# One expert layer's token rows: from selection products to a DRAM buffer and transposes

## The reference, cut to what matters

```python
def moe_swiglu(h, router, wg, wu, wd):
    logits = (h @ router).astype(jnp.float32)
    top_vals, top_idx = lax.top_k(logits, TOP_K)          # TOP_K = 2
    gates = jax.nn.softmax(top_vals, axis=-1)
    gate_e = jnp.sum(jax.nn.one_hot(top_idx, N_EXPERTS) * gates[..., None], axis=-2)
    out = jnp.zeros_like(h)
    for e in range(N_EXPERTS):                            # 8 experts, D_FF = 3584
        out = out + gate_e[..., e:e + 1] * swiglu(h, wg[e], wu[e], wd[e])
    return out
```

## Time and profile before

| | us |
|---|---|
| median of 3 runs | 2628.06 (2624.84 to 2633.0) |
| span of the profiled execution | 2626.9 |
| PE busy | 2533.8 |
| DVE busy | 1814.5 |
| ACT busy | 1450.9 |
| mean DMA rate over the span | 240 GB/s |

### The profile page before, as it was taken

The page is one execution under the profiler, slowest core; times in us unless marked ns, Lnnn a source line. Parts: engine busy times, 40 slices in busy tenths (PEclk is TensorE's granted clock), DMA queues, the critical chain, the costliest instruction groups (busy, mean ns, idle before and its releaser), DMA issues.

```text
span 2626.9 us, 33515 instructions
## 1 busy us (share of the span) xinstructions
PE 2533.8 (96%) x11951; PEld 2014.9 (77%) x11951; DVE 1814.5 (69%) x1779; ACT 1450.9 (55%) x1613; POOL 51.7 (2%) x40
## 2 busy tenths in 40 slices
PE   7999999889999999999999999999999999998998
PEld 6678887667888888888888787888884688777787
DVE  6565446648898989888888985645444575777544
ACT  4553434647777777676767775445433343466443
POOL 0000000000000000000000000600000000000000
PEclk9999999989999999999999999999999999999999
DMA  6865543759999999999999996655534344435661
GB/s 218 310 222 187 189 162 107 262 185 385 348 361 344 360 347 358 340 365 335 372 335 369 325 344 208 226 189 186 188 132 137 95 131 133 133 106 170 200 192 64
DMA packets 327742, 631.65 MB, mean 240 GB/s; under 512 B 14088, under 2 KB 112936, under 8 KB 327464
## 3 DMA queue, kind: packets, MB, share of 16 engines
q1 hardware_dynamic: 326792, 627.35, 68.7%
q0 software_dynamic: 864, 3.15, 0.3%
HBM read 629.40 MB, written 1.05 MB: 240 GB/s over the span
## 4 chain that ended last, share of the span: by engine, by line
PE 87%; DVE 6%; ACT 4%; issue 2%; DMA 1%; SPq 0%; DVEq 0%; ACTq 0%
PE ps L904 21%; PE ps L830 19%; PE ps L934 11%; PE ps L859 9%; PE ps L1304 6%; PE ps L764 5%; PE ps L1331 2%; PE ps L1236 2%; DVE As L2302 1%; PE ps L959 1%; PE ps L1039 1%; PE ps L919 1%; PE ps L843 1%; PE ps L1295 1%; ACT As L1696 1%
## 5 line engine op out<-in xcount | busy, mean ns | idle before, releaser
L2302 DVE TENSOR_TENSOR As<-ringA,As 128x2048 fp32r<-128x2048 f32 x318 | 732.9, 2305 | 224.8 <-ACT As L1613 131.9
L904 PE MATMUL ps<-As,xgs 128*128 128x512 f32 x2688 | 660.7, 396 | 5.7 <-DVE As L2302 3.0
L904 PEld LDWEIGHTS ps<-As,xgs 128*128 128x128 f32 x2688 | 495.0, 188 | 112.0 <-issue 5.8
L1696 ACT ACTIVATE As<-ringA 128x2048 fp32r<-128x2048 f32 x224 | 428.8, 1914 | 28.3 <-PE ps L904 28.1
L830 PE MATMUL ps<-As,xs 128*128 128x512 f32 x1456 | 377.8, 398 | 3.9 <-DVE hh L2339 3.9
L934 PE MATMUL ps<-Bs,hds 128*128 128x512 f32 x1332 | 322.9, 391 | 4.7 <-DVE hds L2365 1.9
L830 PEld LDWEIGHTS ps<-As,xs 128*128 128x128 f32 x1456 | 273.2, 190 | 63.6 <-DVE hh L2339 4.8
L934 PEld LDWEIGHTS ps<-Bs,hds 128*128 128x128 f32 x1332 | 248.2, 188 | 63.0 <-issue 9.7
L2384 DVE TENSOR_TENSOR Bs<-ringB,Bs 128x2048 fp32r<-128x2048 f32 x111 | 254.0, 2289 | 7.3 <-ACT Bs L1726 4.9
L859 PE MATMUL ps<-Bs,hds 128*128 128x512 f32 x1056 | 247.9, 390 | 0.0
L1726 ACT ACTIVATE Bs<-ringB 128x2048 fp32r<-128x2048 f32 x111 | 213.1, 1920 | 62.1 <-PE ps L934 62.1
(11 more groups left out here) (390 smaller groups left out, 3276.9 us busy)
## 6 DMA issues: line engine op xcount, KB each, us to landing
ringA<-in_moe_w_gate SPq DMA_DIRECT2D x112, 1024.0 KB, 5.1
ringA<-in_moe_w_up SPq DMA_DIRECT2D x112, 1024.0 KB, 5.2
ringB<-in_moe_w_down SPq DMA_DIRECT2D x112, 1024.0 KB, 5.4
ringA<-in_w_ff_in SPq DMA_DIRECT2D x132, 512.0 KB, 4.7
ringA<-in_w_in SPq DMA_DIRECT2D x56, 1024.0 KB, 5.3
ringA<-in_w_ada SPq DMA_DIRECT2D x36, 1024.0 KB, 6.2
ringB<-in_w_ff_out SPq DMA_DIRECT2D x33, 1024.0 KB, 5.0
ringA<-in_dense_w_gate SPq DMA_DIRECT2D x28, 512.0 KB, 3.7
```

The source lines that it names most:

```text
L904: m = mm(ps[:, bank, :], lhs(l, tt, k), As[:, h, r, k % 4, :], start=k == 0 and n == 0, stop=k == KC - 1 and n == 2)
L1696: A(As[:, h, 0, :, :], ringA[:, (p["a"] + u) % 2, 4 * h:4 * h + 4, :], ACT.Copy).then_inc(A_high, 1)
L2302: V.tensor_tensor(As[:, h, 1, :, :], ringA[:, (p["a"] + u) % 2, 4 * h:4 * h + 4, :], f32(As[:, h, 0, :, :]), ALU.subtract).then_inc(A_spli ...
```

## The change

The chosen rows of experts 1 to 7 are no longer computed. A DRAM buffer `taken` holds (8 + 1) * 128 rows of 1024. POOL fills it with zeros by nine DMAs, behind the first layer's attention (`o_done` at 4). In expert 0's block 3, DVE works out in `places` for each token and each of its two choices the row `e * 128 + slot`, and POOL then writes the token rows there by four indirect DMAs (2 choices, 2 tiles). SP waits for these (`put`) once, in expert 0. In experts 0 to 6, behind the loads of pair i = 3, SP loads the next expert's 128 rows into `xrow`, which is `xn[:, 0, :]`. At the gather's old place PE turns these rows with 8 transposes. Expert 0's own rows are still made by the products. `one_hot` for `sel` is done for expert 0 alone.

```diff
         most = sb("most", [P, 1], I32)
+        place = sb("place", [P, 2 * TILES], U32)
+        taken = nc.dram_tensor("taken", ((NE + 1) * P, D), F32, kind="Internal").ap()
         AR_N = 18688
...
         chosen = ar(2816, TILES, NE)
+        xrow = xn[:, 0, :]
+        blank = ar(18192, 256)
         sgW, hhW = (hT[:, k:k + 4, :].rearrange("p k n -> p (k n)").rearrange("p (t n) -> p t n", t=TILES) for k in (0, 4))
...
         slot_mm, most_ready, col_ready, sel_ready, selg_ready = (sem(n) for n in ("slot_mm", "most_ready", "col_ready", "sel_ready", "selg_ready"))
+        cleared, placed, put, rows_back = (sem(n) for n in ("cleared", "placed", "put", "rows_back"))
         gathered, xg_ready, selg_tp, selgT_ready, mixed_back, added = (sem(n) for n in ("gathered", "xg_ready", "selg_tp", "selgT_ready", "mixed_back", "added"))
...
                     for h in range(2):
-                        if isinstance(e, int) and isinstance(i, int) and i == 0:
+                        if isinstance(e, int) and e == 0 and isinstance(i, int) and i == 0:
                             half_free(a0, h)
...
-                def rest(e):
-                    with sp.Fori(1, nb // 2) as i:
+                def pairs_of(e, first, last):
+                    with sp.Fori(first, last) as i:
                         for u in range(2):
...
+                def rows_of_next(e):
+
+                    sp.wait_ge(tile_done, e * (2 * nb) + (p["td"] + 2))
+                    sp.dma_start(xrow, taken[bass.ds(e * P + P, P), :]).then_inc(rows_back, 16)
+
+                def rest(e):
+                    pairs_of(e, 1, 4)
+                    if isinstance(e, int) and e == 0:
+                        sp.wait_ge(put, 16 * 2 * TILES)
+                    rows_of_next(e)
+                    pairs_of(e, 4, nb // 2)
+
+                def start(e):
+                    for u in range(2):
+                        A(e, 0, u)
+                        B(e - 1, nb // 2 - 1, u)
+
...
                 rest(0)
-                with sp.Fori(1, NE) as e:
-                    for u in range(2):
-                        A(e, 0, u)
-                        B(e - 1, nb // 2 - 1, u)
+                with sp.Fori(1, NE - 1) as e:
+                    start(e)
                     rest(e)
+                start(NE - 1)
+                pairs_of(NE - 1, 1, nb // 2)
                 B(NE - 1, nb // 2 - 1, 0)
...
-            def gather(e):
-
-                pe.wait_ge(sel_ready, e + 1)
-                if not isinstance(e, int) or e >= 2:
-                    pe.wait_ge(added, 2 * e - 2)
+            def gather_first():
+
+                pe.wait_ge(sel_ready, 1)
                 for half in range(2):
...
                             last = mm(ps[:, 6 + half, k * P:(k + 1) * P], xn[:, tt, o:o + P], sel[:, tt, :], start=tt == 0, stop=tt == TILES - 1)
+                    last.then_inc(gathered, 1)
+
+            def turn_taken(e):
+
+                pe.wait_ge(rows_back, 16 * e)
+                if not isinstance(e, int) or e >= 2:
+                    pe.wait_ge(added, 2 * e - 2)
+                for half in range(2):
+                    for k in range(4):
+                        o = (4 * half + k) * P
+                        last = tr(ps[:, 6 + half, k * P:(k + 1) * P], xrow[:, o:o + P], ident)
                     last.then_inc(gathered, 1)
...
                         if not final:
-                            gather(e + 1)
+                            turn_taken(e + 1)
...
             with pe.If(pe.value_load(most[0:1, 0:1], min_val=0, max_val=SEQ) < CAP + 1):
-                gather(0)
+                gather_first()
                 expert(0)
...
+            ch.done(G.memset(blank, 0.0))
+            pool.wait_ge(o_done, 4)
+            for g in range(NE + 1):
+                pool.dma_start(taken[g * P:(g + 1) * P, :].rearrange("p (a b) -> p a b", a=4), blank.unsqueeze(1).broadcast_to([P, 4, 256])).then_inc(cleared, 16)
             pool.wait_ge(vt_copied, 1)
...
+            pool.wait_ge(cleared, 16 * (NE + 1))
+            pool.wait_ge(pn_xn, PN["ffn1"]["xn"] + 2)
+            pool.wait_ge(placed, 4)
+            for j in range(2 * TILES):
+                pool.indirect_dma_start(out=taken[:, :], out_offset=bass.IndirectOffsetOnAxis(ap=place[:, j:j + 1], axis=0), in_=xn[:, j % 2, :], in_offset=None).then_inc(put, 16)
             pool.wait_ge(spread_copied, units_before(NADA))
...
                 all_tokens(NE - 1)
+                act.wait_ge(rows_back, 16 * (NE - 1))
                 for h in range(2):
...
+            def places():
+
+                at, hit, to = small[:, 400:416].rearrange("p (t e) -> p t e", t=TILES), small[:, 416:448].rearrange("p (j e) -> p j e", j=2 * TILES), small[:, 448:452]
+                for tt in range(TILES):
+                    last = V.scalar_tensor_tensor(at[:, tt, :], k1("iota")[:, 0:NE], float(P), slots[:, :, tt], ALU.mult, ALU.add)
+                last.then_inc(placed, 1)
+                dve.wait_ge(placed, 1)
+                for j in range(2 * TILES):
+                    last = V.scalar_tensor_tensor(hit[:, j, :], k1("iota")[:, 0:NE], ixf[:, j % 2, j // 2:j // 2 + 1], at[:, j % 2, :], ALU.is_equal, ALU.mult)
+                last.then_inc(placed, 1)
+                dve.wait_ge(placed, 2)
+                V.tensor_reduce(to, hit, X, ALU.add).then_inc(placed, 1)
+                dve.wait_ge(placed, 3)
+                V.tensor_copy(place[:, :], to).then_inc(placed, 1)
+
...
                         add(e - 1, 0)
+                    if n == 3 and first:
+                        places()
                     if n == 4:
...
                             dve.wait_ge(selg_tp, e)
-                        one_hot(e, 2 * e + 2, True)
-                    if n == 5 and not final:
-                        dve.wait_ge(gathered, 2 * e + 2)
-                        one_hot(e + 1, 2 * e + 3, False)
+                        one_hot(e, e + 2, True)
                     if n == NB1 - 2 and not final:
...
             with dve.Else():
+                places()
+
```

## The result

| | before | after |
|---|---|---|
| median of 6 runs each, us | 2631.78 (2624.84 to 2635.82) | 2612.11 (2607.39 to 2618.61) |
| span of the profiled execution | 2626.9 | 2606.0 |
| PE busy | 2533.8 | 2511.2 |
| DVE busy | 1814.5 | 1811.8 |
| POOL busy | 51.7 | 67.0 |

The ratio is 0.9936 with a 95% interval of 0.9920 to 0.9952: 16.8 us less, between 12.6 and 21. The prediction said 13.3 us less.

The account below looks back on a forecast made before the run. PE was taken as the bound, busy 96% of the span, with DVE and the DMA engines close. 17.3 - 2.5 - 0.5 - 1.0 = 13.3 us less turned the median of 2628.06 into 2614.8 us, range 2608 to 2625.

Parts of the forecast that it names:

- seven boundaries: At the gathers of experts 1 to 7, transposes replacing products save 2.47 us each, 17.3 us in all.
- row loads: Each expert's 0.52 MB load delays SP's later weight loads 1.36 us, hidden by the ring's lead: 0, uncovered 9.5 us.
- clearing: Nine zeroing DMAs behind the first attention partly meet the first dense loads: 2.5 us lost, bounds 0 and 3.6.
- `places`: Eight short DVE instructions behind expert 0's block 3: 0.5 us lost, bounds 0 and 1.6.
- `put`: SP's wait in expert 0 for the indirect writes holds up the weight loads queued behind it: 1.0 us lost.
- DVE's two idle spells: At each gather, DVE's idle 1.16 us (hidden tile) and 1.31 us (weight part) go when PE is earlier.
- the DMA stream is the real bound: Rival: loads over the experts set the pace, leaving a gain of 3.8 us, 2624.3 us; chance 0.09.
- 3.5 MB in the free time: Of the clearing's 4.7 MB, the part that moves in free DMA time from 128 to 145 us.
- `put` somewhat late: Rival: POOL's four indirect issues in expert 0 wait behind DVE, `put` 9.2 us later, 2624.0 us; chance 0.11.
- the lead of 7.4: Time in us from a weight load's landing to its need, by which loads can be late without costing PE.
- the slower rival: Slow indirect DMA issues in expert 0 hold SP at `put`; at 15 us each the kernel takes 2648; chance 0.07.
- DVE keeps its place: Rival: at the gathers DVE's idle for ACT stays, leaving 4.1 us gained, 2624.0 us; chance 0.05.
- The change doesn't do what it says: Rival: the kernel takes the branch for all tokens, so the edited gather isn't the one run; no own chance given.

Follow-up runs that it names:

- run 9: Changed kernel, clearing moved behind the dense stage with seven DMAs, and expert 0's wait for `put` and row load two pairs later: 2610.4 us, ratio 0.9931.
- runs 2 to 6: Changed kernel with, in order: selection products kept, 2633.0 us; later clearing, 2607.51; two transposes, 2613.78; `dispatch` on ACT, 2619.61; these last two together, 2612.67.
- run 1: Kernel before, with transposes of the first 128 rows replacing experts 1 to 7's products and none of the new DMAs: 2607.04 us, ratio 0.9930.
- run 8: Changed kernel with three, in another kernel seven, further 0.52 MB DMAs behind each row load: 2617.24 us with three, 2656.55 us with seven.
- run 7: Changed kernel, with POOL waiting for seven more blocks of the expert layer before its indirect DMAs: 2628.3 us.

## Why the prediction was right, step by step

| step | predicted, us | measured, us |
|---|---|---|
| seven boundaries | -17.3 (2.47 each) | -19.0 (2.72 each) |
| row loads | 0 | 0 (125.15 to 125.19 with, 125.13 to 125.23 without) |
| clearing | +2.5 | +2.7 (2.1 to 3.3 at expert 0's first product) |
| `places` | +0.5 | at most +0.55 (expert 0 of run 9 less before) |
| `put` | +1.0 | +1.1 (after less run 9, expert 0; 0.3 to 1.5 with the others) |
| sum | -13.3 | -14.6 |

`places` and `put` each rest on one execution of run 9. Six kernels run the same expert 0 (after, runs 2 to 6), and it takes 109.19 to 110.42 us in them, so the two terms together are 0.8 to 2.1 us, where 1.5 was predicted.

**The boundary.** The mechanism held: PE's product time leaves, DVE's two idle spells close, and the release by `xgs` moves by 15.60 - 12.96 = 2.64 us. The size was a little low on both sides. Eight transposes followed by a product hold PE for 0.79 us, not 0.88 (two with their tail) or 1.04 (the last one's end counted), so PE gives 2.70. On DVE, two spells of 1.16 and 1.31 make 2.47, but when nothing is idle between two instructions they also overlap by some 0.08 us each (697.08 + 0.41 = 697.49, yet the next starts at 697.41), which makes 2.64. An idle spell in the trace is a little shorter than what closing it returns. The period gives 2.72 us; where the last 0.08 lie wasn't found. That the missing `one_hot` is worth nothing wasn't tested by itself: it went together with the products in every run.

**The loads.** That the row loads cost nothing is shown by runs 1, 2 and 8. The rival "the DMA stream is the real bound" falls, though the share now reads 1.00: a share of 1.00 at 366 GB/s still left room for four times the row load, and the stream became the bound at 378 GB/s (run 8).

The Trainium skill (DMA: Bandwidth & Descriptors, "Issuing engines are not separate DMA queues") has all issuers on the same 16 engines. The trace agrees: POOL's clearing made a load of SP's 2.7 us later. The landings tell it too; while the indirect writes ran, from 619 to 632 us, these are issues and the time from issue to landing:

```profile
ringA<-in_moe_w_up SPq DMA_DIRECT2D x2, 1024.0 KB, 10.7
ringB<-in_moe_w_down SPq DMA_DIRECT2D x1, 1024.0 KB, 11.5
```

Before it was 5.3 us.

**The clearing.** 3.5 MB in the free time were predicted. The queues from 128 to 145 us (packets, MB, share) show POOL's:

```profile
q0 software_dynamic: 972, 3.58, 53.0%
```

The other 1.1 MB met the first dense load.

**`put`.** The term came out right, by two errors that cancel. I had priced the issue of an indirect DMA by a plain one, 0.77 us, so 3.1 us for four. They took 9.0 us (619.64 to 628.64). The rival "`put` somewhat late" had named just this, with 9.2 us on top; 5.9 came. But the delay of the stream was overstated. I had it 9.4 us late from 628.25 on, although in my own working POOL was through with its issues at 620.8; that left 7.4 us in which the data could move, and the late issues fell into them. By 628.6, the end of the last issue, 0.62 of the 2.1 MB had moved. In run 9, where SP isn't held at this place, the load in question goes out 628.11 - 578.70 = 49.4 us behind expert 0's first product, before the change 628.25 - 579.45 = 48.8, and after it 637.99 - 580.78 = 57.2 us: 7.8 to 8.4 us late, little more than the lead of 7.4. So the size of this term is luck: 5.9 us of late issue cost next to nothing of their own, and run 7 shows that the next ones would have. The price of the slower rival at 15 us an issue, 2648, doesn't follow from its own steps either: `put` at 677.7 is 42 us behind 635.7, 14.3 of them are gained elsewhere, and 2628.06 + 27.7 = 2655.8.

**DVE keeps its place** fell with the two idle spells. **The change doesn't do what it says** fell with the rows of 8 transposes.

**What stays open.** The measured parts sum to -14.6 us and the ratio gives -16.8 us; the 2.2 us between them are inside the interval. Whether they come from the clock's lower level, whose stretches lie elsewhere in every run, wasn't tried. What such a stretch costs can be estimated: from the first dense load to expert 0's first product, run 1 has 428.43 us with 17.1 at the lower level, run 9 433.50 with 30.7, and neither has the clearing ahead, so it is 0.37 us for each. By that the 6.9 us behind the experts make 2.6 of the profiled pair's 4.9; the rest is open too.

## What to carry to other kernels

Read a step's price on every engine that has to pass the same point. Here DVE's own run and the way through PE and ACT stood within 0.07 us of each other once the gather was short, and a further cut on PE or on DVE alone bought nothing. A busy DMA stream is not yet a bound: the lead of the ring, read as the time from landing to need, says how large a burst is free, as long as the stream as a whole has room; and a share of 1.00 doesn't say whether it has. And where an effect of 3 us is looked for in a kernel whose runs spread by 10, compare the parts in the trace, not the medians.

## What the runs showed of the hardware

**An indirect DMA's issue waits for DVE's splits.** DVE's timeline beside POOL's four issues above:

```profile
618.99 2.28 DVE L2343 TENSOR_TENSOR As<-ringA,As 128x2048 fp32r<-128x2048 f32 x1
621.46 2.29 DVE L2343 TENSOR_TENSOR As<-ringA,As 128x2048 fp32r<-128x2048 f32 x1 [0.19 <-ACT As L1736]
624.26 2.29 DVE L2425 TENSOR_TENSOR Bs<-ringB,Bs 128x2048 fp32r<-128x2048 f32 x1 [0.51 <-ACT Bs L1766]
...
627.76 2.29 DVE L2343 TENSOR_TENSOR As<-ringA,As 128x2048 fp32r<-128x2048 f32 x1
```

These splits end at 621.27, 623.75 and 626.55; the issues end at 622.24, 624.60 and 627.38, so 0.97, 0.85 and 0.83 us behind. The fourth issue begins at 627.69, just ahead of the next split, and takes 0.95 us. In run 7 the issues fall elsewhere, and the fourth begins inside a split that ends at 648.56:

```profile
638.66 2.33 POOL L1541 DMA_INDIRECT taken<-xn,place  x1 [102.36 <-DVE As L2344]
641.29 2.93 POOL L1541 DMA_INDIRECT taken<-xn,place  x1 [0.30 <-issue]
644.53 2.66 POOL L1541 DMA_INDIRECT taken<-xn,place  x1 [0.30 <-issue]
647.49 1.90 POOL L1541 DMA_INDIRECT taken<-xn,place  x1 [0.30 <-issue]
```

It takes 1.90 us there, until 649.39, again 0.83 us behind the split's end; the other three end 0.96, 0.85 and 0.83 us behind theirs. So an issue is some 0.9 us of work, and what lies above that is DVE's. The nine plain issues of the clearing weren't held so, with a split of DVE of the same kind, from 129.16 to 131.45, in their midst: 6.88 us for nine, 0.76 each, is the price of the earlier trace rows.

```profile
128.38 6.88 POOL L1522 DMA_DIRECT2D taken<-arena  x9 [127.34 <-DVE arena L2696]
```

The Trainium skill (SBUF — State Buffer, "SBUF: two separate sides") describes the port that DVE and GpSimd share as an exclusive lock, and says that a DVE instruction with two inputs in SBUF takes it against a GpSimd operation that reads SBUF. The trace fits that for POOL: a split reads `ringA` and `As`, and the indirect DMA reads `place`, whereas the plain ones read no indices and weren't held. The reverse isn't seen: the split that begins at 627.76, 0.07 us behind the fourth issue, takes its 2.29 us. So that it is this port is argued from the coincidence of the times, not shown by an edit of its own. The warning that the prediction took from this section was for any DMA that GpSimd issues; the nine plain ones don't bear it out beside such a split.
